# Rebuilding a router between two stages of a decoder step: logits by token, a slot table from one-hots, gates behind the indices

## The chip, the core and the metric

One NeuronCore of a Trainium2 chip runs the whole program. The metric is the device time of one execution in microseconds (us). PE is TensorE, DVE is VectorE, ACT is ScalarE, POOL is GpSimd, SP is SyncE.

## The reference

Two layers of a decoder trunk over 256 prompt tokens and 8 x 4 sample tokens (288 tokens, width 1024, float32). Each layer adds a mixer (RG-LRU, convolution and retention groups between `w_in` and `w_out`) and then a mixture of experts. The change is in the second part:

```python
def hier_moe(x, wg, bg, we, be, w1, w3, w2):      # x is rmsnorm(x, norm_ffn_g)
    pg = softmax(xf @ wg + bg)                     # 4 groups
    g_sel = argmax(pg); p_top = pg[g_sel]
    le = (xf @ we + be).reshape(-1, 4, 8)          # 8 experts in each group
    top_v, top_i = top_k(le[g_sel], 2)
    pe = softmax(top_v)
    eid = g_sel * 8 + top_i
    gates = sum(one_hot(eid, 32) * (p_top * pe))
    # over all 32 experts: y += gates[:, e] * ((silu(x @ w1[e]) * (x @ w3[e])) @ w2[e])
```

## The kernel before, in words

The tokens stand in three tiles, t = 0 and 1 with 128 tokens each and t = 2 with the 32 sample tokens. Everything is static: each engine has its own hand-written instruction order, and engines meet only by semaphores. Each of the eight PSUM banks is handed round by a written plan (`bank_plan`); `start`, `done`, `full`, `free` and `freed` are the waits and increments on a bank's two counters.

Where this text speaks of the router it means, in each layer, the stretch from the last matmuls with `w_out` to the first matmul of the experts. Its order before the change:

1. `mixed(t, h)` (L857) multiplies the mixer's output with `w_out` for tile t and half h; DVE adds it to `x` (L1486). ACT then takes the mean square and its root (L1730, L1731), DVE the reciprocal (L1158) and scales the rows (L1164). PE transposes the scaled rows (`norm`, L619), and DVE multiplies with the norm's weights while it empties the bank (`turned`, L1173). On PE the order is: tile 1's first half of `mixed`, tile 0's transposes, tile 1's second half, tile 2's transposes, the logits of tiles 0 and 2, tile 1's transposes, the logits of tile 1. ACT also issues the stores of the scaled rows to a scratch tensor in HBM (`store_rows`, L1861).
2. The logits (L894) come out as 36 rows by 288 tokens: the router's weights are the stationary operand (36 columns), the tokens move. ACT adds the bias (L1871), and three more transposes bring the logits to tokens by 36.
3. DVE picks group and experts (L1508 to L1530) and marks each choice in a one-hot. `osumb` (L1532) is the sum of the two one-hots. From it PE counts, with triangular and all-one matrices, how many earlier tokens chose each expert (the bank `cum`, L924).
4. DVE first computes the gates (L1535 to L1541), then handles the overflow: an expert has 64 slots, and tokens beyond them go to one of 8 overflow blocks. The number of a token's slot (L1547 to L1561) is split in a place inside the block and a block (L1563 to L1567). POOL marks the place in a one-hot of 128 columns (L1976, six instructions), DVE marks the block, times the token's number or its gate, in one of 40 columns (L1571, twelve instructions). Six matmuls (L936, twelve records) of the two give a table, slot by block, of token number and gate. DVE copies it out and turns it to integers (L1586 to L1592): `gidx`.
5. POOL gathers the rows of 128 slots (two experts) from the scratch tensor by `gidx` with an indirect DMA (L1989). PE transposes them (`tokens`) and the experts begin: `up` (L973), `turn_h`, `down` (L999), `give_back` (L1021, L1027, L1012), sixteen pairs of experts in a layer, with the loads of the next experts' weights (L481, L485, L489) on SP's queue, each released by the matmuls that read the place in the ring before.

While PE waits in the router it multiplies the identity with itself (`keep_clock`, L625), a written number of times in each of three places: `WAIT_CHOICE` before the counts, `WAIT_MARKS` before the table, `WAIT_ROWS` before the gathered rows. PE's queue is in order, so these must end before what stands behind them. In the trace each float32 matmul is two records.

The last expert's `w2` of each layer goes to spare tiles that the router uses too (L567). At the very start of the program ACT issues four small loads, among them the router's biases, and DVE waits for all four before its first instruction on the tokens.

Of the kernel before, what the change touches and what calls it, by code (L numbers as in the profile page):

```python
# [25 lines left out]
I32 = mybir.dt.int32  # L26
# [24 lines left out]
WAIT_NORM, WAIT_CHOICE, WAIT_MARKS, WAIT_ROWS = (13, 8), 17, 26, 17  # L51
# [7 lines left out]
for _name, _k in PARAMS:  # L59
# [6 lines left out]
          ("sin", 96), ("iota", 128), ("first", NBLK), ("ovc", 32),  # L66
          ("thr", 4), ("iotaj", 8), ("desc", 4), ("vals", 6)]
# [7 lines left out]
def constants():  # L75
# [42 lines left out]
    e = np.arange(NE)  # L118
    put("iota", np.tile(np.arange(128), (128, 1)))
    put("first", np.tile(SLOTS * np.arange(NBLK), (128, 1)))  # L120
    put("ovc", np.tile(SLOTS * (NE - 1 - e), (128, 1)))
# [3 lines left out]
    put("vals", (2 * (p[:, None, None] + 128 * np.arange(3)[None, :, None]) + np.arange(2) - OUTSIDE).reshape(128, 6))  # L125
# [4 lines left out]
def bank_plan():  # L130
# [9 lines left out]
    jobs += [("w2", 1), ("w10", 2), ("n2t0a", 3), ("n2t0b", 5), ("w11", 4), ("n2t2a", 6), ("lgT", 7),  # L140
             ("n2t1a", 0), ("n2t1b", 3)]
    jobs += [("lg", 2), ("cum", 5), ("tab", 6)]
# [37 lines left out]
def build(nc, ins, outs):  # L180
# [10 lines left out]
    with ExitStack() as ctx:  # L191
# [32 lines left out]
        lbias = sb("lbias", [NG + NE, DEPTH])  # L224
# [59 lines left out]
        bsum = krf[:, 384:480].rearrange("p (t e) -> p t e", t=3)  # L284
        ge = krf[:, 480:576].rearrange("p (t e) -> p t e", t=3)
        ovcmp = krf[:, 576:832]
        lgT = krf[0:NG + NE, 832:832 + NT]
# [16 lines left out]
        gate, slot, slotu = cut((3, 2)), cut((3, 2)), cut((3, 2), U32)  # L304
        slot_in, slot_blk = cut((3, 2)), cut((3, 2))

        sel, selu, gidx, tok = cut((2, NPAIR + OVER)), cut((NPAIR + OVER,), U32), cut((NPAIR + OVER,), U32), cut((3, NPAIR + OVER))
# [10 lines left out]
        slot_oh = vf[:, 0:768].rearrange("p (t k s) -> p t k s", t=3, k=2)  # L318
        blk_oh = vf[:, 768:768 + 12 * NBLK].rearrange("p (t k v b) -> p t k v b", t=3, k=2, v=2)
# [23 lines left out]
        def bc(a, shape):  # L343
# [7 lines left out]
        bd_in, wr_in, g_in, gfin_in = (sem(f"{n}_in") for n in ("bd", "wr", "g", "gfin"))  # L351
# [15 lines left out]
        lg_arg, lg_exp, osum_ready, mark_ready, idx_ready, back_ready = (  # L367
            sem(n) for n in ("lg_arg", "lg_exp", "osum_ready", "mark_ready", "idx_ready", "back_ready"))
# [3 lines left out]
        eps_ready, slot_ready, slot_marked = sem("eps_ready"), sem("slot_ready"), sem("slot_marked")  # L372
# [78 lines left out]
        def _(sp):  # L451
# [40 lines left out]
            for l in range(DEPTH):  # L492
# [65 lines left out]
                full(sp, l, "lgT")  # L558
# [5 lines left out]
                for i in range(2):  # L564
                    sp.wait_ge(gath[i], 16 * (l * GROUPS + 1))
                for f in range(2):
                    sp.dma_start(spare_w2[f], w2[l, NE - 1, 128 * f:128 * f + 128, :]).then_inc(spare2_in, 16)  # L567
                for it in range(1, GROUPS):
                    for pair in range(2):

                        experts = [u for u in (2 * pair, 2 * pair + 1) if 4 * it + u < NE - 1]
                        for u in experts:
                            xfull(sp, "h", u, it - 1, l)
                            expert(l, it, u)
                        xfull(sp, "y1", pair, it - 1, l)
                        for u in experts:
                            expert2(l, it, u)

                sp.wait_ge(idx_ready, l + 1)
# [27 lines left out]
        def _(pe):  # L607
# [19 lines left out]
            def norm(l, s, t):  # L627
# [5 lines left out]
                pe.wait_ge(rows_ready, norm_turn(l, s, t))  # L633
                r = rows[0:n, t % 2, :].rearrange("p (m k) -> p m k", k=KT)
# [21 lines left out]
            for l in range(DEPTH):  # L656
# [235 lines left out]
                def logits(o, n):  # L892
                    for k in range(KT):
                        i = pe.matmul(bank("lgT")[0:NG + NE, o:o + n], wr[:, k, :], uTk[:, k, o:o + n], start=k == 0, stop=k == KT - 1)  # L894
                    return i
# [4 lines left out]
                mixed(1, 1, (0, 1, 4, 5, 6, 7, 2, 3))  # L900
                norm(l, 1, 2)
                pe.wait_ge(wr_in, 32 * (l + 1))
                freed(pe, l, "n2t0b")
                start(l, "lgT")
                logits(0, 128)
                freed(pe, l, "n2t2a")
                logits(SEQ, NT - SEQ)
                norm(l, 1, 1)
                freed(pe, l, "n2t1b")
                done(logits(128, 128), "lgT")  # L910
                freed(pe, l, "lgT")
                b = start(l, "lg")[:, 0:3 * (NG + NE)].rearrange("p (t e) -> p t e", t=3)
                for t, (o, n) in enumerate(TILES):
                    i = transpose(b[0:n, t, :], lgT[:, o:o + n], NG + NE)
                done(i, "lg")
# [13 lines left out]
                b = start(l, "tab")  # L929
                keep_clock(b, WAIT_MARKS)  # L930
                b = b[:, 0:2 * NBLK]
                for t, (o, n) in enumerate(TILES):
                    pe.wait_ge(mark_ready, 3 * l + t + 1)
                    pe.wait_ge(slot_marked, 3 * l + t + 1)
                    for k in range(2):
                        i = pe.matmul(b, slot_oh[0:n, t, k, :], blk_oh[0:n, t, k, :, :], start=(t, k) == (0, 0), stop=(t, k) == (2, 1))  # L936
                done(i, "tab")
# [93 lines left out]
                def experts4(it, first=False, last=False):  # L1031
                    for pair in range(2):
# [13 lines left out]
                        down(pair, it, spare=last and pair == 1)  # L1046

# [997 lines left out]
```

## Time and profile before

| | before |
|---|---|
| median of 3 runs | 909.07 us (908.74 to 909.43) |
| the profiled execution | 908.88 us |
| its span, first to last instruction | 907.0 us |
| mean granted PE clock | 0.991 |
| busy share of the span: PE, DVE, ACT, POOL | 95%, 59%, 19%, 15% |
| first pair of experts' rows at PE, layer 0 and layer 1 | 193.76 us, 640.36 us |

The profile gives each engine's instructions with start and duration, by line of the kernel. Times in the rows are us from the first instruction of the span. In a line of the timeline, the bracket at the end is the idle time of that engine ahead of the line and what ended it. Lines for PEld are PE's loads of the stationary operand, which run beside its matmuls; a matmul's end is modelled.

### The profile page before, as it was taken

The numbers are of one execution on the slowest core, as the hardware profiler recorded it, in microseconds if no ns is written. First come the engines' busy times: TensorE is split into PE (matmuls) and PEld (weight loads), VectorE is DVE, ScalarE is ACT, GpSimd is POOL, SyncE is SP. The second block draws the span as 40 slices with busy tenths as digits, with TensorE's granted clock in tenths as the row PEclk, the third lists the DMA queues.
The fourth block names the chain that finished last, engine by engine and source line by source line (L and its number), as shares of the span: only waits on it lengthen the run. The fifth ranks groups of instructions, "written<-read, shape, count | busy, mean of one in ns | idle before, by whom it ended". The sixth has DMA issues, their size and how long they took to land.

```text
span 907.0 us, 14885 instructions
## 1 busy us (share of the span) xinstructions
PE 859.5 (95%) x5580; PEld 493.2 (54%) x5612; DVE 533.6 (59%) x1205; ACT 173.3 (19%) x357; POOL 132.6 (15%) x217
## 2 busy tenths in 40 slices
PE   7999999989999999999799999998899999999994
PEld 6745544765555555555377445448655555555551
DVE  2468986535565555646624789946256555564656
ACT  2304113102111111111311121311111111111113
POOL 0101030041121111211010011201312111121100
PEclk9999999999999999999999999999999999999998
DMA  9961933849999999992973047355699999999821
GB/s 289 313 239 65 313 98 89 282 162 414 377 416 412 416 400 401 413 413 110 329 229 139 1 188 184 98 168 215 249 398 403 413 417 413 417 397 392 355 71 53
DMA packets 100881, 252.79 MB, mean 279 GB/s; under 512 B 31682, under 2 KB 65494, under 8 KB 84438
## 3 DMA queue, kind: packets, MB, share of 16 engines
q1 hardware_dynamic: 94890, 244.67, 72.1%
q0 software_dynamic: 4608, 4.73, 1.6%
q10 hardware_dynamic: 1340, 2.80, 0.8%
q8 instruction: 28, 0.46, 0.2%
q14 instruction: 15, 0.12, 0.0%
HBM read 258.13 MB, written 6.52 MB: 292 GB/s over the span
## 4 chain that ended last, share of the span: by engine, by line
PE 77%; issue 12%; DVE 7%; DMA 1%; POOL 1%; ACT 1%; DVEq 0%; SPq 0%; POOLq 0%; ACTq 0%
PE psum L973 25%; PE psum L999 13%; PE psum L688 12%; PE psum L667 7%; PE psum L619 5%; PE psum L1027 5%; PE psum L1021 3%; DVE x L1638 3%; PE psum L1012 2%; PE psum L699 2%; PE psum L625 1%; DMA rows<-xn_scratch,sg 1%; PE psum L755 1%; POOL v L1976 1%; DVE uT L1173 1%
## 5 line engine op out<-in xcount | busy, mean ns | idle before, releaser
L973 PE MATMUL psum<-ring,arena 128*64 128x256 f32 x1984 | 226.4, 381 | 2.4 <-DVE arena L1608 2.4
L973 PEld LDWEIGHTS psum<-ring,arena 128*64 128x64 f32 x1984 | 141.6, 137 | 85.7 <-issue 24.8
L1638 DVE TENSOR_TENSOR x<-x,psum 128x512 f32<-128x512 f32 x128 | 82.2, 684 | 160.7 <-PE psum L1027 160.5
L999 PE MATMUL psum<-ring,arena 128*64 128x512 f32 x496 | 116.9, 599 | 2.4 <-DVE arena L1618 2.4
L688 PE MATMUL psum<-ring,uT 128*128 128x512 f32 x256 | 113.0, 596 | 0.0
L1998 POOL TENSOR_SCALAR kT<-const,sg 128x128 bf16<-128x128 f32 (+1 forms) x96 | 49.2, 522 | 360.9 <-PE psum L1012 360.7
L688 PEld LDWEIGHTS psum<-ring,uT 128*128 128x128 f32 x256 | 47.8, 190 | 55.2 <-issue 54.4
L1626 DVE TENSOR_TENSOR v<-arena 128x512 f32<-128x512 f32 x64 | 44.3, 693 | 46.1 <-ACT arena L1882 46.1
L1882 ACT ACTIVATE arena<-psum,sg 128x512 f32<-128x512 f32 x64 | 44.0, 687 | 138.1 <-PE psum L999 138.1
L1889 ACT ACTIVATE arena<-psum 128x256 f32<-128x256 f32 x64 | 24.5, 383 | 236.4 <-PE psum L973 236.4
L999 PEld LDWEIGHTS psum<-ring,arena 128*64 128x64 f32 x496 | 34.3, 137 | 60.7 <-issue 57.3
L667 PE MATMUL psum<-uT,ring 128*128 128x288 f32 x256 | 63.2, 408 | 1.0 <-DVE uT L1173 1.0
L857 PE MATMUL psum<-ring,mixT 128*128 128x512 f32 x128 | 57.0, 596 | 0.0
L667 PEld LDWEIGHTS psum<-uT,ring 128*128 128x128 f32 x256 | 48.3, 190 | 14.1 <-DVE uT L1173 1.3
L1642 DVE TENSOR_TENSOR x<-x,psum 32x256 f32<-32x256 f32 x128 | 52.9, 413 | 1.4
L619 PE MATMUL psum<-const,rows 128*128 128x128 f32 (+1 forms) x352 | 49.4, 284 | 3.1 <-DVE rows L1164 1.8
L1248 DVE SCALAR_TENSOR_TENSOR cb<-glp,prm,cb 128x256 f32<-128x256 f32 x120 | 51.8, 505 | 0.5 <-DVE hst L1389 0.4
L1027 PE MATMUL psum<-v,kT 128*128 128x512 bf16 x128 | 49.6, 388 | 1.9 <-DVE kT L1629 1.9
L619 PEld LDWEIGHTS psum<-const,rows 128*128 128x128 f32 (+1 forms) x352 | 42.5, 193 | 12.5 <-issue 8.6
L1027 PE MATMUL psum<-kT 128*128 128x512 bf16 x128 | 48.3, 377 | 0.0
L1608 DVE TENSOR_TENSOR arena<-psum,gff 128x512 f32<-128x512 f32 x64 | 41.2, 686 | 11.9 <-PE psum L619 11.0
L625 PE MATMUL psum<-const 128*128 128x128 f32 x282 | 40.8, 315 | 7.1 <-DMA const<-in_constants 4.8
(280 smaller groups left out, 865.4 us busy)
## 6 DMA issues: line engine op xcount, KB each, us to landing
ring<-in_moe_w SPq DMA_DIRECT2D x186, 1024.0 KB, 9.5
ring<-in_w_in SPq DMA_DIRECT2D x24, 1024.0 KB, 11.8
ring<-in_w_out SPq DMA_DIRECT2D x8, 1024.0 KB, 7.9
arena<-in_state_ret SPq DMA_DIRECT2D x16, 128.0 KB, 6.1
out<-arena SPq DMA_DIRECT2D x16, 128.0 KB, 2.5
xn_scratch<-rows ACTq DMA_DIRECT2D x4, 512.0 KB, 4.8
uT<-in_moe_w SPq DMA_DIRECT2D x2, 1024.0 KB, 6.9
mixT<-in_moe_w SPq DMA_DIRECT2D x2, 1024.0 KB, 9.5
```

Source lines behind the costliest of these rows:

```text
L619: return pe.transpose(out, in_, ident[0:n, 0:n])
L625: pe.matmul(b[:, 0:128], ident, ident)
L667: i = pe.matmul(b, w[:, k, 128 * (c % 2):128 * (c % 2) + 128], uTk[:, k, :], start=k == 0, stop=k == KT - 1)
L688: i = pe.matmul(b, uTk[:, k, 128 * t:128 * t + 128], w[:, :, k, :], start=k == 0, stop=k == KT - 1)
L857: i = pe.matmul(b, mixT[:, k, 128 * t:128 * t + 128], w[:, :, k, :], start=k == 0, stop=k == 3, skip_group_check=True)
L973: i = pe.matmul(b[64 * j:64 * j + 64, 0:FE], xsT[:, u // 2, k, s], w[j][:, k, :], start=k == 0, stop=k == KT - 1, skip_group_check=True)
L999: i = pe.matmul(b[64 * q:64 * q + 64, :], hT[:, q, f, :], w[:, 512 * j:512 * j + 512], start=f == 0, stop=f == 1, skip_group_check=True)
L1027: i = pe.matmul(b, back[:, pair, 64 * (a - a % 2):64 * (a - a % 2) + 128], y[:, 512 * (a % 2):512 * (a % 2) + 512], start=False, stop=y is ...
L1248: chain[c] = own(STT(dst, glp[:, c, k:k + SEQ], w, dst, ALU.mult, ALU.add))
L1638: i = T(s, s, psum[:, b, :], ALU.add)
L1642: i = T(s, s, psum[32 * q:32 * q + 32, b, 0:256], ALU.add)
L1998: own(pool.tensor_scalar(back[:, g % 2, o:o + n], C("iota")[:, 0:n], tok[:, t, g:g + 1], None, ALU.is_equal))
```

## The change

The logits are computed with the tokens as the stationary operand, tile by tile, so that they come out as tokens by 36. The transposes ahead of them read the unscaled `x`, without a wait for the mean square, and DVE scales by the reciprocal and adds the bias when it empties the bank. The rows that are stored to HBM are now scaled on ACT. The logits of tiles 0 and 2 stand in the middle of `mixed(1, 1)`. The slot table is built in the form in which the gather reads it, 128 slots by 16 pairs of experts, from one one-hot of the rank and two of the experts (times token number, and times gate): two groups of twelve matmuls with 16 columns each. The gates' six instructions, and two that multiply them into a one-hot, come behind the indices. The overflow is handled on DVE behind the first gathered rows, with six matmuls of its own behind the first `down`. POOL marks nothing any more. `WAIT_CHOICE` and `WAIT_MARKS` are smaller, `WAIT_ROWS` is as before. The load of the last expert's `w2` moves behind the loads of the second round of experts.

```diff
-WAIT_NORM, WAIT_CHOICE, WAIT_MARKS, WAIT_ROWS = (13, 8), 17, 26, 17
+WAIT_NORM, WAIT_CHOICE, WAIT_MARKS, WAIT_ROWS = (13, 8), 14, 5, 17
@@ sync
-                full(sp, l, "lgT")
+                full(sp, l, "lgb")
...
-                for i in range(2):
-                    sp.wait_ge(gath[i], 16 * (l * GROUPS + 1))
-                for f in range(2):
-                    sp.dma_start(spare_w2[f], w2[l, NE - 1, 128 * f:128 * f + 128, :]).then_inc(spare2_in, 16)
...
+                        if (it, pair) == (1, 1):
+                            sp.wait_ge(idx_ready, l + 1)
+                            for f in range(2):
+                                sp.dma_start(spare_w2[f], w2[l, NE - 1, 128 * f:128 * f + 128, :]).then_inc(spare2_in, 16)
@@ tensor
+                def logits(t):
+                    o, n = TILES[t]
+                    freed(pe, l, f"n2t{t}{'b' if t < 2 else 'a'}")
+                    b = bank("lg") if t == 2 else start(l, ("lg", "lgb")[t])
                     for k in range(KT):
-                        i = pe.matmul(bank("lgT")[0:NG + NE, o:o + n], wr[:, k, :], uTk[:, k, o:o + n], ...)
+                        i = pe.matmul(b[0:n, 36 * t:36 * t + 36], uTk[:, k, o:o + n], wr[:, k, :], ...)
...
                 norm(l, 1, 0)
-                mixed(1, 1, (0, 1, 4, 5, 6, 7, 2, 3))
                 norm(l, 1, 2)
+                mixed(1, 1, (0, 1, 4, 5))
                 pe.wait_ge(wr_in, 32 * (l + 1))
+                logits(0)
+                logits(2)
+                mixed(1, 1, (6, 7, 2, 3))
                 norm(l, 1, 1)
+                logits(1)
...
+                def table(b_, what):
+                    for h in range(2):
+                        b = b_[64 * h:64 * h + 64, 0:NPAIR]
+                        for t, (_, n) in enumerate(TILES):
+                            for k in range(2):
+                                i = pe.matmul(b, slot_oh[0:n, t, k, :], what[0:n, t, k, h:NE:2], ...)
+                    return i
...
+                keep_clock(start(l, "tab"), WAIT_MARKS)
+                pe.wait_ge(tok_marked, l + 1)
+                pe.wait_ge(slot_marked, l + 1)
+                done(table(bank("tab"), tok_oh), "tab")
+                pe.wait_ge(gate_marked, l + 1)
+                done(table(start(l, "tabg"), gate_oh), "tabg")
...
                         down(pair, it, spare=last and pair == 1)
+                        if first and pair == 0:
+                            pe.wait_ge(over_marked, l + 1)
+                            table_over()
@@ vector
                 T(osumb[:, :, :], onehot[:, :, 0, :], onehot[:, :, 1, :], ALU.add).then_inc(osum_ready, 1)
+                for k in range(2):
+                    i = T(tok_oh[:, :, k, :], onehot[:, :, k, :], bc(C("tokv").unsqueeze(2), [128, 3, NE]), ALU.mult)
...
+                full(dve, l, "cum")
+                for k in range(2):
+                    own(T(rtmp[:, :, k, :], onehot[:, :, k, :], cum[:, 0:3, :], ALU.mult))
+                own.wait()
+                do(dve.tensor_reduce(rank[:, :, :], rtmp, AX, ALU.add))
+                in_slots(slot_oh, rank).then_inc(slot_marked, 1)
+                full(dve, l, "tab")
+                free(S(gidx[:, 0:NPAIR], bank("tab")[:, 0:NPAIR], float(OUTSIDE), None, ALU.add), "tab")
...
+                for k in range(2):
+                    i = T(gate_oh[:, :, k, :], onehot[:, :, k, :], bc(gate[:, :, k].unsqueeze(2), [128, 3, NE]), ALU.mult)
...
                 tokens(0, 0)
+                overs()
                 experts4(0, first=True)
...
+                        if first and pair:
+                            overs_marked()
@@ scalar
-            act.dma_start(lbias[0:NG, :], b_grp.rearrange("l g -> g l"), ...).then_inc(g_in, 16)
+            act.dma_start(lbias[:, :, 0:NG], b_grp.partition_broadcast(128)).then_inc(bias_in, 16)
...
+                    A(rows[0:n, t % 2, :], x[0:n, t, :], ACT.Copy, scale=rec[0:n, t:t + 1]).then_inc(rows_ready, 1)
...
-                free(A(lgT, bank("lgT")[0:NG + NE, 0:NT], ACT.Identity, bias=lbias[:, l:l + 1]), "lgT")
@@ gpsimd
-                pool.wait_ge(slot_ready, l + 1)
...
-                pool.wait_ge(idx_ready, l + 1)
+                freed(pool, l, "tab")
                 for t in range(3):
                     pool.wait_ge(xn_out[t], 16 * (l + 1))
```

`overs()` is 26 instructions on DVE: the overflow counts, the place and block of the overflow tokens, their one-hots and values. `overs_marked()` waits for the overflow's table, is seven instructions and increments `idx_ready`, on which SP, PE, ACT and POOL wait only later.

## Rows read from the trace of the kernel before

**Rows 1.** Busy time by stretch: two experts' pair in layer 1.
```profile
core 0: us, PE busy (x) PEld busy (x) DVE busy (x) ACT busy (x) POOL busy (x), PEclk, DMA share, GB/s
661.70:677.40 15.70, 15.41 (x118) 8.30 (x116) 9.00 (x19) 2.69 (x6) 2.77 (x5) 1.00 1.00 404
```
**Rows 2.** Timeline, layer 1, `w_out` to the choice: start, us, engine, line.
```profile
605.45 7.03 PE L857 MATMUL psum<-ring,mixT 128*128 128x512 f32 x16
...
612.41 1.06 PE L619 MATMUL psum<-const,rows 32*128 32x32 f32 x8
...
612.51 0.69 DVE L1486 TENSOR_TENSOR x<-x,psum 128x512 f32<-128x512 f32 x1 [5.04 <-PE psum L857]
...
613.29 1.06 ACT L1730 ACTIVATE tt<-x 128x1024 f32<-128x1024 f32 x1 [11.50 <-DVE x L1486]
613.40 2.38 PEld L894 LDWEIGHTS psum<-uT,wr 128*36 128x36 f32 x32
...
615.82 1.16 PE L619 MATMUL psum<-const,rows 128*128 128x128 f32 x8
616.58 1.29 DVE L1173 TENSOR_TENSOR uT<-psum,gff 128x512 f32<-128x512 f32 x2 [0.82 <-PE psum L619]
617.92 1.67 PEld L894 LDWEIGHTS psum<-uT,wr 128*36 128x36 f32 x16 [1.12 <-DVE uT L1173]
617.92 1.94 PE L894 MATMUL psum<-uT,wr 128*36 128x128 f32 x16 [0.93 <-DVE uT L1173]
...
620.72 4.06 PE L625 MATMUL psum<-const 128*128 128x128 f32 x34
620.83 0.17 DVE L1508 TENSOR_REDUCE sg<-psum 128x3 f32<-128x12 f32 x1 [2.96 <-PE psum L619]
```
**Rows 3.** Timeline, layer 1, from `osumb` to the first gathered rows at PE.
```profile
624.18 0.26 DVE L1532 TENSOR_TENSOR osumb<-kr 128x96 bf16<-128x96 f32 x1
...
624.95 0.33 PE L924 MATMUL psum<-osumb,onesb 128*128 128x32 bf16 x3
...
627.98 0.43 DVE L1559 TENSOR_TENSOR kr<-kr 128x96 f32<-128x96 f32 x2
628.44 0.35 DVE L1561 TENSOR_REDUCE sg<-kr 128x6 f32<-128x192 f32 x1
...
632.12 0.64 PE L936 MATMUL psum<-v 128*128 128x80 f32 x4 [0.43 <-POOL v L1976]
...
634.13 5.69 PE L625 MATMUL psum<-const 128*128 128x128 f32 x34
...
635.10 0.18 DVE L1592 TENSOR_SCALAR sg<-sg 128x24 uint32<-128x24 uint32 x1
...
636.08 1.10 POOL L1989 DMA_INDIRECT rows<-xn_scratch,sg  x1 [2.66 <-DVE sg L1592]
...
640.36 1.16 PE L619 MATMUL psum<-const,rows 128*128 128x128 f32 x8 [0.54 <-DMA rows<-xn_scratch,sg]
```
**Rows 4.** Busy time by stretch, layer 1, around the last dummies (PEclk is sixth).
```profile
636.00:638.00 2.00, 2.00 (x12) 2.00 (x11) 0.00 (x0) 0.00 (x0) 1.62 (x2) 0.50 0.03 6
```
**Rows 5.** Timeline, layer 1, first two experts.
```profile
648.04 0.29 DVE L1618 SCALAR_TENSOR_TENSOR arena<-arena,psum 128x128 f32<-128x128 f32 x1
...
652.30 0.29 DVE L1616 SCALAR_TENSOR_TENSOR arena<-arena,psum 128x128 f32<-128x128 f32 x1 [3.97 <-ACT arena L1895]
...
653.14 0.23 PEld L999 LDWEIGHTS psum<-ring,arena 128*64 128x64 f32 x4 [0.56 <-issue]
```
**Rows 6.** The scratch tensor's DMAs, stores and gathers of both layers, issue to landing.
```profile
DMA to landing us min/median/max: 2.6/7.4/8.9
```
**Rows 7.** Busy time by stretch, layer 0, as the table is built.
```profile
182.00:184.00 2.00, 2.00 (x20) 2.00 (x19) 1.74 (x9) 0.00 (x0) 1.29 (x3) 1.00 0.56 234
```
**Rows 8.** Timeline at the program's start.
```profile
4.82 5.61 PE L625 MATMUL psum<-const 128*128 128x128 f32 x26 [4.82 <-DMA const<-in_constants]
...
8.79 0.75 DVE L1164 TENSOR_SCALAR rows<-x,rec 128x1024 f32<-128x1024 f32 x1
```

More of the change, by code:

```diff
@@ L1566, in _ @@
-                dve.sem_inc(slot_ready, 1)
-                do(T(slot_blk[:, :, :], slot[:, :, :], slot_in[:, :, :], ALU.subtract))
-                for t, (o, n) in enumerate(TILES):
-                    for k in range(2):
-                        for v_, what in enumerate((C("vals", n)[:, 2 * t + k:2 * t + k + 1], gate[0:n, t, k:k + 1])):
-                            i = S(blk_oh[0:n, t, k, v_, :], C("first", n), slot_blk[0:n, t, k:k + 1], what, ALU.is_equal, ALU.mult)
-                            if not (k and v_):
-                                own(i)
-                    i.then_inc(mark_ready, 1)
@@ L1583, in _ @@
-                by_pair = tab[:, :, 0:NE].rearrange("p v (g i) -> p v g i", i=2)
-                for i in range(2):
-                    h = slice(64 * i, 64 * i + 64)
-                    own(dve.tensor_copy(sel[h, :, 0:NPAIR], by_pair[h, :, :, i]))
-                free(dve.tensor_copy(sel[:, :, NPAIR:], tab[:, :, NE:NBLK]), "tab")
-                freed(dve, l, "tab")
-                own.wait()
-                do(S(selu[:, :], sel[:, 0, :], float(OUTSIDE), None, ALU.add))
-                S(gidx[:, :], selu[:, :], 1, None, ALU.logical_shift_right).then_inc(idx_ready, 1)
@@ L1593, in _ @@
-                dve.wait_ge(idx_ready, l + 1)
-                do(dve.tensor_copy(tok[:, 0, :], gidx[:, :]))
-                for t in (1, 2):
-                    own(S(tok[:, t, :], tok[:, 0, :], float(-128 * t), None, ALU.add))
-                own.wait()
-                dve.sem_inc(tok_ready, 1)
+                do(T(gate[:, :, 1], gate[:, :, 0], r_e2[:, :], ALU.mult))
+                for k in range(2):
+                    i = T(gate_oh[:, :, k, :], onehot[:, :, k, :], bc(gate[:, :, k].unsqueeze(2), [128, 3, NE]), ALU.mult)
+                    i.then_inc(gate_marked, 1) if k else own(i)
@@ new lines, in _, with token_of @@
+                freed(dve, l, "tab")
+                def token_of(a, b):
+                    do(dve.tensor_copy(tok[:, 0, a:b], gidx[:, a:b]))
+                    for t in (1, 2):
+                        own(S(tok[:, t, a:b], tok[:, 0, a:b], float(-128 * t), None, ALU.add))
+                    own.wait()
+                token_of(0, NPAIR)
+                dve.sem_inc(tok_ready, 1)
+                full(dve, l, "tabg")
+                free(dve.tensor_copy(sel[:, 0:NPAIR], bank("tabg")[:, 0:NPAIR]), "tabg")
@@ new lines, in overs_marked @@
+                def overs_marked():
+                    full(dve, l, "tabo")
+                    own(dve.memset(gidx[64:128, NPAIR:], OUTSIDE))
+                    own(dve.memset(sel[64:128, NPAIR:], 0.0))
+                    own(S(gidx[0:64, NPAIR:], bank("tabo")[0:64, 0:OVER], float(OUTSIDE), None, ALU.add))
+                    free(dve.tensor_copy(sel[0:64, NPAIR:], bank("tabo")[0:64, OVER:2 * OVER]), "tabo")
+                    freed(dve, l, "tabo")
+                    own.wait()
+                    token_of(NPAIR, NPAIR + OVER)
+                    dve.sem_inc(idx_ready, 1)
```

221 lines of the change are left out of this document (117 added, 104 removed).

## The prediction

> **What bounds the kernel now.** I read the mean granted clock first (0.991, so one steady machine), then busy time by stretch, then the chain of waits, then the timeline of the router in both layers; the layers repeat each other within 0.3 us, so I work on layer 1 and count twice. In the experts' stretch PE is busy 15.41 of 15.70 us for each pair, at full clock, and every one of the fifteen pairs behind the first takes the same time [rows 1]. DMA's share there is 1.00 too, but PE waits for no weights: the loads follow PE. So whatever the router gives up is kept to the end, and what is put on PE there is paid. In the router nothing runs at its peak: it is a chain from `mixed(1, 1)` over logits, choice, counts, table, indices and gather to the first transposes at 640.36 [rows 2, 3]. That moment, per layer, is all that the sum is about. I call O the end of `osumb`, 624.44 before, G the end of the last instruction on `gidx`, 635.28 before, and P the first rows at PE, 640.36 [rows 3]: P is O + 15.92.
>
> **Logits by token.** Before, PE filled its waits with the logits of tiles 0 and 2. Now these and tile 2's transposes stand ahead of the end of `mixed(1, 1)`, which was 612.48 [rows 2]. The transposes cost 1.06. For tile 0 the stationary operand is now 128 columns wide; a 128-wide record costs 4.06/34 = 0.119 as the dummies do, or 1.67/16 = 0.104 as tile 1's do; I take 0.114. 16 records are 1.82. Tile 2's 32-wide records: (2.38 - 1.67)/16 = 0.044, so 0.71 [rows 2]. `mixed(1, 1)` ends at 612.48 + 1.06 + 1.82 + 0.71 = 616.07. Then DVE's addition 0.69; transposes without the wait for the mean square; the first half is 0.76 later (615.82 to 616.58); DVE 1.29; logits 1.82 and 0.27 for the last one to come out (1.94 - 1.67); with five handoffs of 0.03 to 0.05 the logits of tile 1 end at 621.04. The bank is emptied with scale and bias in about 0.2, and the choice begins at 621.28 against 620.83: **0.45 later**. So the wait of 3.3 for square, root and scaling and the detour over ACT and three transposes are gone, and nearly all is given back, since PE's fill work now is in the way. Bounds: 0.1 (0.104 and shorter handoffs) to 0.9. The choice itself is the same work: O is 624.89.
>
> **From O to G.** The counts end 0.84 after O (625.28); the two products with `tokv` (0.43) hide under them. Two products with the counts 0.43, the reduction 0.35 [rows 3]. The one-hot has 384 elements: between 0.22 for 96 (half of 0.43) and 0.69 for 512, so 0.55 [rows 2, 3]. The table is twelve matmuls, 24 records, of 64 stationary and 16 moving columns, which the trace doesn't show. Bounds: 0.044 as for 36 columns, 0.119 as for 128. Loads of 64 columns in `down` start some 0.03 apart (four loads in 0.23 altogether) [rows 5], so I take a value near the low end, 0.057, half of 0.114: 1.37, and 0.27 to come out. The copy to integers is 0.18. With 0.16 of handoffs that is 4.15 against 10.84 before: **6.69 less**. Bounds of the saving: 5.3 to 7.0. What is gone is eighteen instructions of marks on DVE and POOL, the twelve on slot and block, the overflow's eight, the gates' six.
>
> **From G to P.** The gather needs 5.08 from G to the transposes (635.28, issue at 636.08, 640.36) [rows 3]. But PE's queue holds something longer. The gates' six small instructions are 6 x 0.21 = 1.26, their one-hots 0.43 and handoffs 0.08: the second table can start at G + 1.77 and ends at G + 3.2. Behind it stand 17 dummies, the same number as before, when they began 1.15 ahead of G (634.13). They took 5.69 [rows 3], and would begin at G + 3.2: P is G + 8.9, not G + 5.08. **3.8 back**. The 5.69 holds a piece at half clock: the 34 records before the counts took 4.06 [rows 2], and from 636 to 638 the granted clock was 0.50, that is 1.2 GHz, after PE had been fed only short bursts of `tab` matmuls (0.64 each, a microsecond apart) [rows 3, 4]. Afterwards it was back at 2.4. In the changed kernel the thin stretch is longer, from O + 2.3 to G + 3.2, some 5 us with two tables in it; so I take 5.69 again.
>
> **The overflow.** `overs()` stands on DVE behind the first rows. It is 26 instructions, 0.21 for the small ones and up to 0.55, about 6.4 in sum. DVE is done with the rows at P + 2.1 (0.76 and 1.29 as for tile 1) [rows 2], so with this at P + 8.5. Behind it waits the first `hidden`, which ended at 648.33, P + 8.0; it will end about 1.1 later. The next of its kind begins at 652.30, P + 11.9 [rows 5], and PE is in the second expert's `up` all that time, so this costs nothing while the slack of 3 us lasts; without it DVE's surplus would be paid in full. `table_over` is on PE: twelve records, 0.057 each, **0.7 paid**. `overs_marked` puts about 1.1 on DVE ahead of `split`; the first `give_back` needs only the top part at once and its PE time moves by 0.7 too, so zero, at most 0.4.
>
> **Moved at no cost.** POOL waits for the three stores of the scaled rows. ACT now scales tile 1's rows after DVE's reciprocal at 618.9, which takes 1.06 as the square did [rows 2], so the store is issued near 620.2. A landing of 7.4, at most 8.9 [rows 6], is 627.6 to 629.1; the gather is issued near 629.8. ACT's other two scalings fall in idle time, and the exponentials are needed only at G. The last `w2` of each layer, 1 MB, now comes among other loads on SP's queue; at 404 GB/s [rows 1] that is 2.6 us of transfer, and each load is issued a whole round (31 us) ahead of its use, so it is hidden; if loads were late already, it would be 2.6 a layer. SP's wait for `idx_ready` comes when that is long past. At the start, the biases are written as many small pieces; the first rows are scaled by 9.54, but PE's dummies last to 10.43 [rows 8]: 0, at most 0.3 more.
>
> **Sum.** -6.69 + 0.45 + 3.8 + 0.7 = -1.74 a layer, -3.5 in all. The profiled execution took 908.88 (its span 907.0, and 1.9 around it), 0.19 under the median 909.07. So the forecast is **905.6**. P should come 13.05 after O.
>
> **Rivals.** (a) *The clock holds.* If the tables keep PE at 2.4 GHz, the dummies take 4.06 and P is G + 7.3: another 1.63 a layer, less in layer 0 where the gather may be later: 902.6. For it: only the tables' own records are changed. Against: before, denser bursts were not enough [rows 3, 4]. (b) *The clock stays down longer.* All 34 records at half clock are 8.1, 2.4 more than I took; half of that gives 908.0, all of it 910.4. For it: the thin stretch is longer than before; against: the dummies themselves brought the clock back. (c) *Small matmuls are dear*, the case on the other side: if each record with 64 stationary columns costs as much as a 128-wide one, 0.114, the first table is 1.37 longer, the second too, and `table_over` 0.68: 3.4 a layer, net 1.7 slower, so 912.4. It decides from the point where 60 records outweigh 1.74, that is at 0.086 a record. For it: the old table's records stood 0.114 apart or more [rows 3]; against: those were 128 wide, and the 36-wide ones took 0.044 [rows 2]. The Trainium skill ("TensorE: Matmul & The Clock Gate", section "LDWEIGHTS (loading the stationary operand)") says the time of a load goes with its columns alone; by its figure 64 columns are 53 ns, an estimate of 1.28 us for 24 records. The rows at 36 and 128 columns agree with that, so it speaks against this rival. (d) *The gather lands late in layer 0.* DMA was still 0.56 busy at 182 to 184 there [rows 7], and the third and fourth expert's loads now begin 3.6 later, so weights are still moving when the gather is issued near 183. If it then takes the 8.9 that gathers among loads take at most [rows 6], P is G + 9.8, 0.9 more, once: 906.5. The Trainium skill ("DMA: Bandwidth & Descriptors", "Issuing engines are not separate DMA queues") has the DMAs of all issuing engines interleave on the same sixteen engines. The longer landings among loads agree; it would make this case likelier in layer 0 and void in layer 1.
>
> **Chances.** Forecast 0.40; (a) 0.14; (b) 0.24; (c) 0.14; (d) 0.08. A measurement of this kernel tells 0.2%, 1.8 us, from no change. Faster is below 907.2: 0.36 of the forecast, all of (a), 0.05 of (b), 0.07 of (d), 0.62. Slower is above 910.9: all but 0.01 of (c), 0.03 of (b), 0.16. The rest is 0.22. The range reaches from (a) with 0.3 to spare, 902.3, over (b) nearly whole, to 909.8; it leaves out (c) and the end of (b). The likeliest case alone, with the bounds of logits and table, is 903.5 to 907.8.
>
> **What would show it.** In the changed profile: L894's successor for tile 1 ending near 621, the choice starting 0.3 to 0.6 later; the indices 4.2 after `osumb`; a first table of about 1.4 us; a granted clock of 0.50 for some 3 us around the second table; the dummies 5 to 6 us long, and the first rows' DMA landed 3 to 4 us before PE turns them; from the second pair on, 15.7 us each. The forecast is wrong if the dummies end before the gather lands, if table records stand over 0.08 apart, or if PE waits for DVE in the first round.

## The result: 915.3 us, slower by 0.55%

The changed kernel took **915.3 us** (median of 4 runs, 914.98 to 915.5) against 908.95 for the kernel before beside it (908.74 to 909.43, 4 runs): ratio 1.0055, 95% interval 1.0035 to 1.0075. The profiled execution took 915.5, its span 913.6 against 907.0, its mean granted clock 0.980 against 0.991. 905.6 was forecast with a range to 909.8, so sign, number and range are all wrong.

The 6.6 us of span come from the very start (5.7) and from the router of both layers (0.3 and 0.57). The timeline of the start in the changed kernel (start, us, engine, line):

```profile
2.25 0.49 ACTq L1796 DMA_DIRECT2D lbias<-in_moe_b_expert  x1
4.00 10.83 SPq L466 DMA_DIRECT2D ring<-in_lru_conv_w  x1
8.24 1.06 ACT L1800 ACTIVATE tt<-x 128x1024 f32<-128x1024 f32 x1 [2.46 <-DMA x<-in_x_prompt]
17.99 3.22 PE L675 MATMUL psum<-uT,ring 128*128 128x288 f32 x6 [4.02 <-DMA ring<-in_w_in]
```

Two of these rows in the kernel before:

```profile
4.00 3.65 SPq L464 DMA_DIRECT2D ring<-in_lru_conv_w  x1
14.66 6.57 PE L667 MATMUL psum<-uT,ring 128*128 128x288 f32 x26 [0.52 <-DVE uT L1173]
```

SP's queue stands 10.83 us on one small load instead of 3.65, and the first `w_in` matmul starts 3.33 later, now because PE waits for the weights. The two loads of `w_in` issued first (at 2.57 and behind) took, before and after:

```profile
DMA to landing us min/median/max: 8.9/10.1/11.2
DMA to landing us min/median/max: 15.3/16.3/17.4
```

The first of them is the one that PE needs: 2.57 + 8.9 is 11.5, some 3.2 before its first matmul at 14.66, and 2.57 + 15.3 is 17.9, just ahead of the matmul at 17.99. The clock is lower as well: 0.90 and 0.93 in the first two stretches of 20 us, 1.00 in both before, and the first group of `w_in` takes 10.24 instead of 7.86. So the transposes behind it start at 28.23 against 22.52, 5.71 late (3.33 of it the wait, 2.38 the clock), and the trace stays 5.7 late up to the router of layer 0. The view of the DMAs in the first 20 us, of the changed kernel (last in a line: median us to landing):

```profile
DMA packets 4030, 3.74 MB, mean 187 GB/s; under 512 B 1209, under 2 KB 3742, under 8 KB 4030
ring<-in_w_in SPq DMA_DIRECT2D x3, 1024.0 KB, 15.3
lbias<-in_moe_b_expert ACTq DMA_DIRECT2D x1, 32.0 KB, 12.0
lbias<-in_moe_b_group ACTq DMA_DIRECT2D x1, 4.0 KB, 8.5
```

and of the kernel before:

```profile
DMA packets 5396, 5.49 MB, mean 275 GB/s; under 512 B 826, under 2 KB 5108, under 8 KB 5396
ring<-in_w_in SPq DMA_DIRECT2D x5, 1024.0 KB, 8.9
```

Two loads of 36 KB together go with a third less traffic for 20 us. The router's timeline in layer 1, answering to [rows 2, 3]:

```profile
607.59 3.17 PE L865 MATMUL psum<-ring,mixT 128*128 128x512 f32 x7
610.60 2.05 PE L621 MATMUL psum<-const,x 128*128 128x128 f32 x16
612.57 3.70 PE L865 MATMUL psum<-ring,mixT 128*128 128x512 f32 x8
616.11 2.51 PE L906 MATMUL psum<-wr,uT 128*128 128x36 f32 x32
618.55 3.70 PE L865 MATMUL psum<-ring,mixT 128*128 128x512 f32 x8
623.08 1.13 PE L621 MATMUL psum<-const,x 128*128 128x128 f32 x8 [0.83 <-issue]
625.14 1.97 PE L906 MATMUL psum<-wr,uT 128*128 128x36 f32 x16 [0.94 <-DVE uT L1199]
626.95 5.00 PE L627 MATMUL psum<-const 128*128 128x128 f32 x28
631.78 0.18 PE L930 MATMUL psum<-osumb,upb 128*128 128x32 bf16 x1
634.02 1.84 PE L941 MATMUL psum<-v 128*64 128x16 f32 x24 [0.27 <-DVE v L1586]
637.68 3.07 PE L941 MATMUL psum<-v 128*64 128x16 f32 x24 [1.82 <-DVE v L1603]
640.68 5.67 PE L627 MATMUL psum<-const 128*128 128x128 f32 x34
646.18 1.04 PE L621 MATMUL psum<-const,rows 128*128 128x128 f32 x8
```

The stretches of 2 us there (PEclk is the third number from the end):

```profile
626.00:628.00 2.00, 2.00 (x15) 2.00 (x15) 0.74 (x5) 1.61 (x2) 0.00 (x0) 0.75 0.98 379
628.00:630.00 2.00, 2.00 (x11) 2.00 (x11) 1.79 (x15) 0.43 (x3) 0.00 (x0) 0.50 0.95 311
638.00:640.00 2.00, 2.00 (x19) 1.93 (x18) 0.23 (x2) 0.00 (x0) 0.99 (x1) 0.50 0.39 86
642.00:644.00 2.00, 2.00 (x11) 2.00 (x11) 0.00 (x0) 0.00 (x0) 0.81 (x3) 0.50 0.00 0
```

PE runs at 1.2 GHz in two stretches: behind its waits around the transposes of tile 1, and from about 637.2 to 644.1. Its gathered rows had long landed: the gather was issued at 636.87, and the view of the tile of gathered rows says

```profile
DMA to landing us min/median/max: 4.0/4.1/4.3
```

so they lay there from 641.2, while PE worked off 34 dummy records, 5.67 us long, until 646.18. In the table O, G and P are as in the prediction; the shift of the work ahead (6.04 in this layer) is taken off the first row.

| layer 1, us | before | predicted | after |
|---|---|---|---|
| choice, against the work ahead | 620.83 | +0.45 | +0.57 |
| O to G | 10.84 | 4.15 | 5.00 |
| G to P | 5.08 | 8.9 | 10.11 |
| O to P | 15.92 | 13.05 | 15.12 |
| the rest of the first round | | +0.7 | +0.8 |
| per layer | | -1.74 | +0.57 |
| start of the program | | 0 to +0.3 | +5.7 |

### The profile page after: what moved, and what is told of

It is laid out like the page before. It is cut to its first block, busy times and chain, and to the rows that moved or that the text cites. A ratio compares the mean times of both kernels' runs of the same rounds, so it can differ in the third digit from the quotient of the medians.

```text
span 913.6 us, 14917 instructions
## 1 busy us (share of the span) xinstructions
PE 867.5 (95%) x5606; PEld 493.2 (54%) x5606; DVE 530.5 (58%) x1215; ACT 179.3 (20%) x361; POOL 125.2 (14%) x205
## 4 chain that ended last, share of the span: by engine, by line
PE 88%; DVE 7%; DMA 2%; issue 1%; ACT 1%; SPq 0%; DVEq 0%; ACTq 0%
PE psum L995 25%; PE psum L1021 13%; PE psum L696 12%; PE psum L675 7%; PE psum L621 6%; PE psum L865 5%; PE psum L1049 5%; PE psum L1043 4%; DVE x L1704 3%; PE psum L627 3%; PE psum L1034 2%; DMA ring<-in_w_in 2%; PE psum L707 2%; PE psum L941 1%; PE psum L906 1%
## 5 line engine op out<-in xcount | busy, mean ns | idle before, releaser
L675 PE MATMUL psum<-uT,ring 128*128 128x288 f32 x256 | 65.5, 418 | 4.5 <-DMA ring<-in_w_in 4.0
L2052 POOL DMA_INDIRECT rows<-xn_scratch,sg x32 | 35.2, 1101 | 124.9 <-DVE sg L1592 92.6
L621 PE MATMUL psum<-const,rows 128*128 128x128 f32 (+1 forms) x304 | 42.7, 284 | 1.9 <-DVE rows L1190 1.9
L1043 PE MATMUL psum<-arena,kT 128*128 128x512 bf16 x128 | 40.7, 393 | 1.7 <-ACT arena L1953 0.9
```

The costliest lines, as they stand in the source:

```text
L621: return pe.transpose(out, in_, ident[0:n, 0:n])
L675: i = pe.matmul(b, w[:, k, 128 * (c % 2):128 * (c % 2) + 128], uTk[:, k, :], start=k == 0, stop=k == KT - 1)
L1043: pe.matmul(banks[-1], back[:, pair, 64 * (a - a % 2):64 * (a - a % 2) + 128], y_top[:, 512 * (a % 2):512 * (a % 2) + 512], start=True, st ...
```

## The experiments

Runs of one batch are compared with runs of the kernel before on the same chip, which spread wider there (907.35 to 913.59) than at first; so small ratios below come with their intervals (95%), and mechanisms are read from the one profiled execution of each kernel. Its time is given where it lies at the edge of the kernel's runs.

**The start, the loads alone.** b1_cast is the kernel before with the two loads added beside its own:

```
+ act.dma_start(extra[:, :, 0:NG], b_grp.partition_broadcast(128)).then_inc(extra_in, 16)
+ act.dma_start(extra[:, :, NG:], b_exp.partition_broadcast(128)).then_inc(extra_in, 16)
```

> The kernel before, with the two broadcast loads of the biases added on ACT's queue at the start (into a part of sg that is free then; nothing uses them). Theory 'one address': the 512 small pieces read the same few bytes of HBM, and everything queued behind them waits; 5.7 us more, about 914.6. Rival 'the start is hidden, the router lost the time': within 0.3 us of before, 909. Rival 'many small pieces': also some 5.7 us more; the next run tells it from the first.

b2_distinct has the same pieces to the same places, but each read from a row of its own of the table of constants:

```
+ far = cst[:, 256:256 + 128].rearrange("p (l g) -> p l g", l=DEPTH)
+ act.dma_start(extra[:, :, 0:NG], far[:, :, 0:NG]).then_inc(extra_in, 16)
+ act.dma_start(extra[:, :, NG:], far[:, :, NG:NG + NE]).then_inc(extra_in, 16)
```

> The same two added loads with as many pieces of the same sizes (256 of 16 bytes, 256 of 128 bytes), but each partition reads its own row of the constants, 6 to 7 KB from the next. Theory 'one address': under 1 us more, 909 to 910. Rival 'many small pieces': 5 to 6 us more, about 914.6, as the run with the broadcast loads.

b1_cast: 913.0 us (10 runs), ratio 1.004 (1.0022 to 1.0058). b2_distinct: 910.33, ratio 1.0008 (0.9993 to 1.0022). The DMA view of the first 20 us of b1_cast, in its fastest execution (909.55):

```profile
DMA packets 4957, 4.57 MB, mean 229 GB/s; under 512 B 1319, under 2 KB 4669, under 8 KB 4957
ring<-in_w_in SPq DMA_DIRECT2D x5, 1024.0 KB, 11.8
```

and of b2_distinct:

```profile
DMA packets 5805, 5.39 MB, mean 270 GB/s; under 512 B 1370, under 2 KB 5517, under 8 KB 5805
ring<-in_w_in SPq DMA_DIRECT2D x5, 1024.0 KB, 9.2
```

The loads alone slow the kernel before by most of what the change lost (0.4% of 0.55%), and the number and size of the pieces is not what does it: with distinct rows as source the weights come almost as before. The first load of `w_in` landed after 12.6 us in b1_cast and 9.2 in b2_distinct, 8.9 before. What is left as the difference is that the pieces of b1_cast all read the same few bytes, or bytes of two small tensors close together; no run tells these two apart, and by which part of the memory system they hold back other loads is not shown. The profiled execution of b1_cast shows the mechanism but not its whole price: its first `w_in` matmul waited 0.74 for the weights and started at 15.29, 0.63 late. Where its other executions lost the rest, no trace shows; their mean granted clock goes down to 0.985, from 0.991 in this one.

**Moved away.** a1_late is the changed kernel with these two loads issued by ACT behind the gate's tanh of tile 1 in layer 0; a2_late_rows3 has also 3 dummies ahead of the gathered rows instead of 17.

```
  group_std(0); gate_tanh(0); gate_tanh(1)
+ if l == 0:
+     act.dma_start(lbias[:, :, 0:NG], b_grp.partition_broadcast(128)).then_inc(bias_in, 16)
+     act.dma_start(lbias[:, :, NG:], b_exp.partition_broadcast(128)).then_inc(bias_in, 16)
- WAIT_ROWS = 17
+ WAIT_ROWS = 3
```

> The changed kernel with its two broadcast loads of the biases issued on ACT behind the tanh of the gates of layer 0, near 125 us, where the profile shows DMA little used, instead of at the start. Theory: the first 37 us are as before, 5.7 us come back: 909.6. Rival 'the loads cost wherever they are': they delay w_out's loads there instead, 912 to 915.

> As the run before it, and WAIT_ROWS 3 instead of 17. The rows of the first gather land 4.9 us before PE turns them (641.2 against 646.18 in layer 1), since 17 dummies stand in PE's queue. Theory 'dummies in the way': the first rows are turned when they land, 4.9 us a layer earlier, less what the low clock costs the first matmuls (under 1.5 us a layer): 901 to 903. Rival 'the dummies earn their time': without them the clock stays at 1.2 GHz into the first up, which takes 3.5 us more a layer, and with the overflow's work nearly all is lost: 907 to 909.

a1_late: 912.23 (8 runs, 908.29 to 915.63), ratio 1.0022 (0.9997 to 1.0047), as the rival had it. The first `w_in` matmul came at 14.01 again, without a wait for weights, but a new wait came up in `w_out` of layer 0:

```profile
138.94 3.24 PE L865 MATMUL psum<-ring,mixT 128*128 128x512 f32 x7 [1.68 <-issue]
```

The loads now ran beside `w_out`'s, which in the stretch from 115 to 142 took 10.9 us to land (6.8 before): by all signs the same harm in another place, though the profile names no releaser for this wait. a2_late_rows3: 906.9 (10 runs), ratio 0.9971 (0.9952 to 0.9989), between theory and rival. Its profile is of its slowest execution, 910.8, against 910.59 of a1_late's, so these two traces do not show the 5.3 between the medians. Its O to P was 10.90 and 11.05, 2.3 and 4.0 less than a1_late, so that much of the dummies' time was of no use; but in layer 0 the first `up` behind them ran at half clock in part, 5.43 for 32 records instead of 3.67. With the rows and the wait ahead of it that gave 2.5 back: in this layer all of the gain.

**A quiet place, and three edits of the router.** c1_idle issues the two loads near 69 us of layer 0, where the DMA queues stand empty; the other three start from it.

```
c1_idle     the two loads behind  A(sg[0:32, 2, :], ..., ACT.Tanh, ...)  if l == 0
c2_order    - mixed(1, 1, (0, 1, 4, 5)); logits(0); logits(2); mixed(1, 1, (6, 7, 2, 3)); norm(l, 1, 1); logits(1)
            + mixed(1, 1, (0, 1, 4, 5, 6, 7, 2, 3)); logits(2); norm(l, 1, 1); logits(0); logits(1)
c3_dummies  WAIT_CHOICE 14 -> 8, WAIT_ROWS 17 -> 4, table_over() ahead of down(0) instead of behind it
c4_all      c2_order and c3_dummies
```

> The change as it is, but layer 0 issues the two broadcast loads of the biases behind the gate's tanh of tile 2 (near 69 us), where the trace shows no DMA traffic. Theory (the loads of small pieces hold back whatever other loads run beside them, and this alone made the start late): the first w_in matmul starts at 14.7 or before, as in the kernel before, and PE waits nowhere for w_out near 138 us, where the load behind the second gate's tanh cost 1.7 us; what is left is the router itself, P - O 15 where the clock falls in front of the counts and back - P 20.6: before within 0.2% (ratio 0.999 to 1.001). Rival (the start is late for another reason, the released g_in or the larger start of the ring): start still 17 to 18 us, ratio 1.005.

> As c1_idle, and in front of the choice PE does all of the second half of w_out for tile 1 first, then the logits of tile 2 (0.5 us), the transposes of tile 1, the logits of tiles 0 and 1; so the logits lie in PE's two waits (0.83 for VectorE's addition, 0.94 for the transposed tile). Theory: the choice starts 1.4 us earlier against the end of the last w_out matmul, the clock does not fall in front of the choice or falls later, and the counts start 0.1 behind osumb instead of 0.6: 1.4 to 2.5 us less per layer than c1_idle, ratio to c1_idle 0.994 to 0.998. Rival (the clock falls after a quiet stretch of its own, wherever the logits lie): only the 1.4 us, and the same low stretch behind the choice.

> As c1_idle, with 8 dummy matmuls in front of the counts instead of 14, 4 behind the second table instead of 17, and the overflow's table in front of the first down pass instead of behind it. Theory (the 34 records at half clock behind the table cost 5 us that the gather does not need): P - O falls from 15 to between 10.5 and 11.5, the counts start with osumb, and PE's 0.39 wait for VectorE before down is filled; against that the first up pass may run at half clock, which cost 1.2 and 2.5 us in a2_late_rows3: 1.5 to 3.5 us less per layer than c1_idle. Rival (the dummies are what keeps the expert passes at full clock): back - P rises by as much as P - O falls, and the ratio to c1_idle is 1.000.

> c2_order and c3_dummies together. Theory (the gains lie in different places): they add, 900 to 905 us where before stands at 909. Rival (both only shift the clock's low stretch): no better than the better of the two.

| | us, median (runs) | ratio to before (95%) | O to P, layers 0 and 1 |
|---|---|---|---|
| c1_idle | 910.52 (11) | 0.9996 (0.9982 to 1.001) | 15.35, 15.21 |
| c2_order | 906.33 (7) | 0.9954 (0.9936 to 0.9973) | 14.18, 15.64 |
| c3_dummies | 907.22 (6) | 0.9959 (0.994 to 0.9978) | 10.66, 12.93 |
| c4_all | 902.89 (4) | 0.9911 (0.9896 to 0.9926) | 12.47, 12.84 |

c1_idle settles the start: its first `w_in` matmul is at 13.72, `w_out` came in 6.3 and PE did not wait for it, and the loss of 0.55% is gone. Not all of the low clock at the start belongs to the loads: c1_idle's first group of `w_in` ran in part at half clock too (9.55), and the transposes behind it started at 23.27. In the nine profiled kernels made from the changed one without the early loads they start between 22.18 and 23.56, against its own 28.23, so of its 5.7 the loads are worth 4.7 at least. What is left of the change, the router itself, is worth nothing that these runs can tell from zero: not the 1.74 a layer of the forecast. The order and the dummies give some 0.4% each, and they add; c3_dummies is three edits at once, and no run separates them. But c4_all came with a surprise: with 8 dummies the clock fell earlier, ahead of the first table, and O to G was 6.00 and 6.36 (4.35 in both layers of c2_order with its 14). c3_dummies had shown it in layer 1 (6.45). Idle time and dummies trade against each other.

**Work laid into PE's waits.** d1_between and d2_choice start from c4_all; both have 16 dummies ahead of the counts, and d1 has dummies also in the wait between the two tables.

```
d1_between  WAIT_CHOICE 8 -> 16, WAIT_ROWS 4 -> 6
            done(table(bank("tab"), tok_oh), "tab")
          + keep_clock(start(l, "tabg"), 7)
            pe.wait_ge(gate_marked, l + 1)
d2_choice   WAIT_CHOICE 8 -> 16
```

> As c4_all, with 16 dummy matmuls in front of the counts instead of 8, 7 in PE's wait of 1.8 us between the two tables where there were none, and 6 behind the second table instead of 4. Theory (the clock falls a few us after PE has stood or done nothing but dummies and tables with waits between them, so work laid into the waits keeps it up): G - O 4.35 in both layers instead of 6.0 and 6.4, the second table at 1.84 instead of 3.07, P - O 10.0 to 10.8 instead of 12.5 and 12.8, 2 to 2.5 us less per layer: 897 to 900 us. Rival (what PE does there does not matter to the clock, as its low stretch comes anyway once per choice): it falls at another point, the 7 dummies take 1.6 or 3.3 us in front of the second table, and the kernel is within 0.2% of c4_all's 0.991, perhaps above it.

> As c4_all, with 16 dummy matmuls in front of the counts instead of 8, nothing between the tables. Theory: as in c2_order with its 14, the clock still stands at 1.0 while the counts and the first table run, so G - O is 4.35 in both layers; the second table runs at half clock as there; P - O 10.8 to 11.3, 1.3 to 1.8 us less per layer than c4_all, ratio to before 0.987 to 0.989. Rival: the low stretch comes as early as in c4_all (its phase, not the number of dummies, decides), G - O stays above 6 in one layer at least, and the ratio stays at 0.991.

d1_between: **893.76 us** (5 runs, 893.5 to 895.52), ratio 0.9824 (0.9806 to 0.9843), better than its theory's 897 to 900. d2_choice: 901.8 (6 runs), ratio 0.9903 (0.9886 to 0.992): O to P is 10.84 and 10.83 as its theory had it, but the ratio is above its range, since the first experts ran at half clock. The timeline of d2_choice, layer 1:

```profile
621.79 1.84 PE L940 MATMUL psum<-v 128*64 128x16 f32 x24 [0.27 <-DVE v L1585]
625.45 3.07 PE L940 MATMUL psum<-v 128*64 128x16 f32 x24 [1.82 <-DVE v L1602]
628.45 2.08 PE L627 MATMUL psum<-const 128*128 128x128 f32 x8
630.32 1.92 PE L621 MATMUL psum<-const,rows 128*128 128x128 f32 x8
633.22 6.01 PE L994 MATMUL psum<-ring,arena 128*64 128x256 f32 x32 [0.98 <-DVE arena L1673]
```

and of d1_between:

```profile
617.86 1.84 PE L940 MATMUL psum<-v 128*64 128x16 f32 x24 [0.27 <-DVE v L1586]
619.62 1.83 PE L627 MATMUL psum<-const 128*128 128x128 f32 x14
621.51 1.87 PE L940 MATMUL psum<-v 128*64 128x16 f32 x24
623.30 1.60 PE L627 MATMUL psum<-const 128*128 128x128 f32 x12
625.01 1.16 PE L621 MATMUL psum<-const,rows 128*128 128x128 f32 x8
627.37 3.67 PE L995 MATMUL psum<-ring,arena 128*64 128x256 f32 x32 [1.20 <-DVE arena L1674]
```

Up to the first table the two are alike. Then d2_choice leaves PE idle for 1.82, and the records from there on are those of half clock: the table 3.07, the rows 1.92, and `up`, real work of the experts, 6.01 instead of 3.67. Two stretches of 2 us of d2_choice, and behind them the one of d1_between in which its second table begins (PEclk is again the third number from the end):

```profile
624.00:626.00 2.00, 0.55 (x5) 0.55 (x6) 1.79 (x10) 0.00 (x0) 1.10 (x1) 0.58 0.00 0
634.00:636.00 2.00, 2.00 (x12) 1.25 (x10) 1.83 (x7) 0.00 (x0) 1.89 (x5) 0.50 0.38 90
```

```profile
620.00:622.00 2.00, 1.94 (x21) 1.75 (x20) 1.79 (x10) 0.00 (x0) 1.10 (x1) 1.00 0.04 16
```

With 14 dummy records in that wait the clock stays at 2.4 GHz through both layers' routers (mean 0.995 over the run against 0.979). P is 9.73 and 9.46 behind O, back to the gather's own length, and the first experts run at full speed. It is 8.0 us for nine dummies a layer, seven in the wait and two behind the second table. The two traces part in the wait, ahead of the second table, so it is the seven that hold the clock; what the two behind add is not measured.

**What it takes, and what the start still costs.** e1_minimal is the changed kernel with the loads moved as in c1_idle, 7 dummies between the tables and 6 behind them, and nothing else. e2_early_bias is d1_between with the loads back at the start.

```
e1_minimal     WAIT_ROWS 17 -> 6, keep_clock(start(l, "tabg"), 7) between the tables, the two loads near 69 us
e2_early_bias  d1_between, the two loads where the change has them
```

> The change with three edits alone: the biases loaded near 69 us of layer 0 (as in c1_idle), 7 of the dummy matmuls behind the second table moved into PE's 1.8 us wait between the tables, 6 left behind it instead of 17 (14 in front of the counts and the order of the logits as they are in the change). Theory A (the 7 dummies between the tables are what kept the clock up in d1_between): the clock falls in front of the counts at most, as PE's waits of 0.83 and 0.94 around the transposes of tile 1 are still there; the second table takes 1.84, P - O is 10 to 11 instead of 15.2, ratio to before 0.987 to 0.990. Theory B (the waits in front decide, and the clock falls there as in c1_idle): it comes back at 632 as in c1_idle, P - O 11.5 to 12.5, ratio 0.991 to 0.994.

> As d1_between, but the two broadcast loads of the biases are at the start, as in the change. Theory: the start costs what it cost the change (first w_in matmul at 17 to 18 us, second group of w_in 5.7 us late in the bad executions, 3 to 5.5 us in the median), and the router gains what it gained in d1_between: 897 to 900 us, ratio to before 0.986 to 0.989. Rival (the delay of the start shifts the phase of the clock and costs more than itself, or part of the 5.5 us was the router's): more than 7 us, or under 2 us, above d1_between.

e1_minimal: 902.69 (6 runs), ratio 0.9915 (0.9895 to 0.9935): the figure of theory B, though P - O (11.07 and 10.32) is nearer to A's. This is read from its fastest execution, 899.86 at a mean clock of 0.992; the others are at 0.986 to 0.990, and no trace shows where they lose. Its timeline in layer 1:

```profile
614.32 1.98 PE L906 MATMUL psum<-wr,uT 128*128 128x36 f32 x16 [0.94 <-DVE uT L1200]
616.13 5.00 PE L627 MATMUL psum<-const 128*128 128x128 f32 x28
...
624.97 1.83 PE L627 MATMUL psum<-const 128*128 128x128 f32 x14
626.86 1.87 PE L941 MATMUL psum<-v 128*64 128x16 f32 x24
```

The second low stretch is gone, the first one (behind the waits of 0.83 and 0.94 in front of the choice) is not. c2_order, which fills them, had its clock at 1.00 until 624 in this layer, with the same 14 dummies. e2_early_bias: 899.81 (5 runs), ratio 0.9873 (0.9849 to 0.9896): 6.0 above d1_between by the medians, 4.5 by the ratios. `w_in` waits 4.08 for its weights again (first matmul 17.45, the transposes behind the group at 27.53 against 22.26), and O to P is as in d1_between (9.67 and 9.35). So start and router are two separate causes, and they add.

## Why the prediction was wrong

- **The step that failed** is the last sentence of *Moved at no cost*: "At the start, the biases are written as many small pieces; the first rows are scaled by 9.54, but PE's dummies last to 10.43 [rows 8]: 0, at most 0.3 more." It measured +5.7 in the profiled execution, +0.4% in b1_cast, and 6.0 by the medians (4.5 by the ratios) between d1_between and e2_early_bias. I priced who waits for the biases (nobody for long) and put at nothing what their loads do to the loads beside them. That term had a bound in the trace of before: the first `w_in` matmul started 3.2 behind the landing of its weights (11.5 to 14.66), so a load slower by more than that is paid by PE. It came 6.4 slower (15.3 instead of 8.9). No rival held this case.
- **Logits by token**: predicted 0.45 later, measured 0.57. Right, and given back for the reason stated: the fill work lies ahead of `mixed(1, 1)`'s end. One reading under it is wrong: the 0.104 was taken for a record with 128 stationary columns, but those records had 36 stationary and 128 moving ones. The records with 36 stationary and 32 moving columns stood 0.044 apart, so the spacing there did not go by the stationary columns alone, as the prediction reads these rows under (c). It did little harm: the loads of tile 1's logits took 1.86/16 = 0.116 each, against the 0.114 that I took. I did not look for the other order, which fills PE's two new waits (0.83, 0.94) and brings the choice forward in c2_order.
- **O to G**: predicted 4.15, measured 5.00 in the changed kernel, 4.35 where the clock held. The table's records stood 1.84/24 = 0.077 apart, not 0.057. By the Trainium skill ("TensorE: Matmul & The Clock Gate", section "LDWEIGHTS (loading the stationary operand)") the estimate was 1.28 for the table. The trace disagrees: the records of the loads alone take 1.77 there. Why, no run shows. The other 0.65 is the counts, kept waiting by 28 dummy records at half clock, 5.00 us (3.37 in c2_order, where the clock held); my working knew only one low stretch, at the tables.
- **G to P**: predicted 8.9, measured 10.11. The idea was right: the dummies, not the gather, set P. The size was off: the second table ran at half clock, 3.07 instead of 1.37 (1.84 at full clock). The prediction did not keep to its own sign here: it expected a granted clock of 0.50 for some 3 us around the second table, and priced the table at full clock. The 5.69 for the 34 records was right to 0.02.
- **Overflow**: 0.7 predicted, 0.8 measured; its 12 records took 0.92. DVE's work behind the rows cost PE nothing, as said.
- **Rivals**: (b), the clock down for longer, is what happened in the router (it had 0.24), though earlier in the chain than it said: at the counts and in the second table, not in the last dummies. (a) did not happen in the change; where the clock holds it is worth more than 1.63 a layer (d2_choice to d1_between is 4.0 a layer), but that took the dummies of d1_between. (c) at full clock did not decide: 0.077 is under its point of 0.086, though (0.077 - 0.057) x 60 records is 1.2 of the 1.74 a layer. In the second table the records stood 0.128 apart, at half clock, which is (b) again. (d) did not happen: layer 0's gather landed in 4.6 at most, and PE turned at 199.03, 9.2 behind its issue.
- Without the start, the forecast's router was some 3.5 us too good: c1_idle stands at 0.9996 (0.9982 to 1.001), the forecast at 0.996. Per layer of the profiled execution it is 0.1 in the choice, 0.85 in O to G, 1.2 in G to P and 0.1 in the first round, and the low clock is 0.65 of O to G and all of G to P. The saving that I claimed is real, 6.4 of O to P in d1_between, but in the change nearly all of it was taken up by the low clock and by dummies whose number had been fitted to the old chain.

## What to carry to other kernels

Price a new load by what it does to the loads beside it, however few bytes it moves, and against the time between the landing of those loads and their use: two small tensors copied to 128 partitions at the start cost some 5 us where the whole redesign was to gain 3.5, and at a moment with empty queues they cost nothing that could be measured. When a chain with timed filler in it gets shorter, fit the filler again: put it into the waits of the engine and not behind the last one, and read the granted clock stretch by stretch after each edit. In these runs a wait of 1 to 2 us on PE could be paid twice, the second time in real work that ran at half speed after it.

## What the runs showed of the hardware

- Two broadcast loads, 36 KB in 512 pieces that read the same few bytes, landed after 8.5 and 12.0 us at the program's start and still after 4.7 and 5.8 with nothing beside them (c1_idle); the first 1 MB load next to them took 15.3 instead of 8.9 (14.8 in e2_early_bias, 12.6 in b1_cast). Another small load's issue held SP's queue for 10.83 instead of 3.65, and for 8.01 in e2_early_bias, but only 3.98 in the fastest execution of b1_cast. With distinct source rows the weights landed in 9.2. The Trainium skill ("DMA: Bandwidth & Descriptors", section "Rules for kernel authors") says that small transfers are mostly overhead and that a source may repeat. What such a source does to other loads is what these runs show.
- PE's idle time weighs more than its amount. In d2_choice the clock fell inside a wait of 1.82 us, with one of 0.27 a table ahead of it, and stayed at 1.2 GHz for some 13.6 us (624.3 to 638.0); with dummies in that wait it never fell. In c4_all idle time ahead of the counts (2.14) did the same one step earlier. The Trainium skill ("TensorE: Matmul & The Clock Gate", section "HAM oscillation — how this bites in real kernels") tells of a kernel whose waits for DMA, longer than any here, throw PE back to the low clock each time. The runs agree in kind, and show it for waits on VectorE of 0.8 to 2.1 us with dummies and small matmuls between them.
- The spread between executions of one kernel goes with the mean granted clock. a1_late's eight runs go from 908.29 at a mean clock of 0.987 to 915.63 at 0.978; d1_between, where it holds, keeps within 893.5 to 895.52, at 0.995 down to 0.993. Why the same kernel meets the low clock more in some executions than in others stays open.
